# First stage of a two-block transformer kernel: 1024-column pieces of the modulation weights, sums of squares on TensorE

## The reference

```python
mod = jax.nn.silu(c) @ ada_w + ada_b                  # c: (1, 1024), ada_w: (1024, 6144)
sh_m, sc_m, g_m, sh_f, sc_f, g_f = jnp.split(mod, 6, axis=-1)
h = rms_norm(x, mix_pre_norm) * (1 + sc_m) + sh_m     # mean of x*x over the 1024 columns
proj = h @ w_in
```

## Time and profile before

| | us |
|---|---|
| median of 3 runs (lowest, highest) | 2764.87 (2758.59, 2766.57) |
| profiled execution, its own time | 2762.08 |
| span of that execution in the trace | 2759.1 |
| PE busy | 2668.9 (97%) |
| start of the stage after the first | 41.5 |

### The profile page before, as it was taken

One profiled execution on the slowest core, in us unless ns is written; L12 is line 12 of the kernel. 1 busy time (PEld: TensorE's weight loads), 2 busy tenths in 40 slices (PEclk: granted clock), 3 DMA queues, 4 the chain that ended last, 5 costly groups with the idle time before them and its releaser, 6 DMA issues. The chain is left out here.

```text
span 2759.1 us, 48978 instructions
## 1 busy us (share of the span) xinstructions
PE 2668.9 (97%) x19134; PEld 2281.0 (83%) x19134; DVE 1884.4 (68%) x3427; ACT 1205.4 (44%) x2294; POOL 285.1 (10%) x217
## 2 busy tenths in 40 slices
PE   7988899999999999999999999999999999999998
PEld 5868766778888789998878999989999857899997
DVE  3454668552332588887457888888888767788885
ACT  3232235531212454445256544465444438654444
POOL 2000114422111300001401000010000100100000
PEclk9999889999999999999999999999999999999999
DMA  8250310123232223334303333332333331323331
GB/s 279 63 169 16 111 38 5 62 77 107 92 95 88 77 77 97 110 92 124 92 17 92 89 104 96 104 107 86 109 99 101 83 86 26 92 79 113 92 108 54
DMA packets 369540, 248.89 MB, mean 90 GB/s; under 512 B 28692, under 2 KB 364376, under 8 KB 369312
## 3 DMA queue, kind: packets, MB, share of 16 engines
q1 hardware_dynamic: 368818, 245.18, 30.2%
q10 hardware_dynamic: 494, 0.59, 0.1%
HBM read 241.52 MB, written 2.12 MB: 88 GB/s over the span
## 5 line engine op out<-in xcount | busy, mean ns | idle before, releaser
L3018 ACT CAST dense_wt_hi<-ring 128x512 fp32r<-128x512 f32 x719 | 444.4, 621 | 462.5 <-PE bank L3068 220.5
L3023 DVE TENSOR_TENSOR dense_wt_lo<-ring,dense_wt_hi 128x512 fp32r<-128x512 f32 x719 | 493.6, 689 | 105.8 <-ACT dense_wt_hi L3018 104.4
L3055 PE MATMUL bank<-dense_operand_hi,dense_wt_hi 128*128 128x256 f32 x1248 | 353.7, 283 | 4.2 <-DVE h L3672 4.2
L3057 PE MATMUL bank<-dense_operand_hi,dense_wt_lo 128*128 128x256 f32 x1248 | 353.1, 283 | 0.0
L3056 PE MATMUL bank<-dense_operand_lo,dense_wt_hi 128*128 128x256 f32 x1248 | 353.1, 283 | 0.0
L3068 PE MATMUL bank<-dense_act_hi,dense_wt_hi 128*128 128x512 f32 x832 | 258.4, 392 | 0.8 <-DVE dense_act_lo L3336 0.8
L3068 PE MATMUL bank<-dense_act_lo,dense_wt_hi 128*128 128x512 f32 x832 | 257.1, 390 | 0.0
L3068 PE MATMUL bank<-dense_act_hi,dense_wt_lo 128*128 128x512 f32 x832 | 256.7, 390 | 0.0
L3055 PE MATMUL bank<-feat_hi,dense_wt_hi 128*128 128x256 f32 (+1 forms) x820 | 246.8, 301 | 7.5 <-DVE h L3707 3.2
L3055 PEld LDWEIGHTS bank<-dense_operand_hi,dense_wt_hi 128*128 128x128 f32 x1248 | 238.8, 191 | 12.2 <-issue 5.0
L3057 PE MATMUL bank<-feat_hi,dense_wt_lo 128*128 128x256 f32 (+1 forms) x820 | 245.8, 300 | 0.0
(11 more groups left out here) (726 smaller groups left out, 5429.3 us busy)
## 6 DMA issues: line engine op xcount, KB each, us to landing
ring<-in_ffn_w_up SPq DMA_DIRECT2D x88, 512.0 KB, 3.9
ring<-in_ffn_w_gate SPq DMA_DIRECT2D x88, 512.0 KB, 5.2
ring<-in_ffn_w_down SPq DMA_DIRECT2D x60, 512.0 KB, 4.8
ring<-in_ada_w SPq DMA_DIRECT2D x24, 1024.0 KB, 8.0
ring<-in_ffn_w_down SPq DMA_DIRECT2D x52, 256.0 KB, 3.9
ring<-in_w_ffn_gate SPq DMA_DIRECT2D x11, 1024.0 KB, 5.3
ring<-in_w_ffn_up SPq DMA_DIRECT2D x11, 1024.0 KB, 5.4
ring<-in_w_in SPq DMA_DIRECT2D x8, 1024.0 KB, 6.5
```

Source lines behind the costliest of these rows:

```text
L3018: self.nc.scalar.copy(self.hi(i), src).then_inc(self.s_high, 1)
L3023: self.nc.vector.tensor_tensor(self.lo(i), self.items[i][1], self.hi(i).bitcast(F32), ALU.subtract).then_inc(self.s_low, 1)
L3055: pe.matmul(out, h[:, w], xh, start=start and k == 0, stop=False, skip_group_check=shared)
L3057: last = pe.matmul(out, l[:, w], xh, start=False, stop=stop and k == 3, skip_group_check=shared)
```

## The change

`FirstModulation` takes the place of `Modulation` in the first stage (the later use of `Modulation` stays). A chunk is now 256 rows by 1024 columns, contiguous pieces of 4 KB; four chunks in a row add up to 1024 of the sums, in one PSUM bank, and a chunk is four products over 512 columns. Two turns of four products each, with two moving columns that pick the rows below and above partition 64, take the place of eight turns of two. DVE clears the two banks in place of the products with zeros. DVE copies all eight tiles of `x`. GpSimd has nothing to do in the stage; PE sums all eight tiles of squares, 32 products. The table of the root is loaded by ACT ahead of its first copy, and the fillers are in other places.

```diff
--- before.py
+++ after.py
@@ -1005,6 +1005,55 @@
             v.tensor_tensor(coef[:, 32:40], mod[:, 40:48], par("ffn_post_norm"), ALU.mult)
 
 
+class FirstModulation:
+
+    def __init__(self, K, st, name, banks, turned):
+        self.K, self.nc, self.banks, self.turned = K, K.nc, banks, turned
+        self.seg = K.plan.segments[name]
+        self.row = st.sb("row", [P, 2, T])
+        self.s_silu, self.s_row, self.s_turned, self.s_clear = st.sems("silu_c", "row_out", "row_turned", "mod_cleared")
+
+    def chunk(self, pe, r):
+        K = self.K
+        K.wait_loaded(pe, self.seg["n0"] + r)
+        w = K.raw(self.seg["n0"] + r).rearrange("p (k n) -> p k n", n=D)
+        for g in range(4):
+            k, half = g % 2, g // 2
+            last = pe.matmul(K.bank[self.banks[r // 4]][32 * g:32 * g + 1, :], K.coef[:, 2 * (r % 4) + k:2 * (r % 4) + k + 1],
+                             w[:, k, half * T:(half + 1) * T], start=r % 4 == 0, stop=r % 4 == 3)
+        last.then_inc(K.tiles_done, 1)
+
+    def turn(self, pe, b):
+        K = self.K
+        pick = K.k("heads").rearrange("p (h d) -> p h d", d=HD)[:, :, 0]
+        pe.wait_ge(self.s_row, b + 1)
+        for j in range(4):
+            last = pe.matmul(K.bank[self.turned][:, 8 * b + j:8 * b + j + 5:4], self.row[:, b, j * P:(j + 1) * P], pick, start=True, stop=True)
+        last.then_inc(self.s_turned, 1)
+
+    def silu(self):
+        K = self.K
+        self.nc.scalar.activation(K.coef[:, 0:8], K.par[:, COL["c"]:COL["c"] + 8], ACT.Silu).then_inc(self.s_silu, 1)
+
+    def clear(self):
+        for b in self.banks:
+            self.nc.vector.memset(self.K.bank[b][:, :], 0.0).then_inc(self.s_clear, 1)
+
+    def row_out(self, act, b):
+        K = self.K
+        act.wait_ge(K.tiles_done, self.seg["mark0"] + 4 * b + 4)
+        self.nc.scalar.copy(self.row[:, b, :], K.bank[self.banks[b]][:, :]).then_inc(self.s_row, 1)
+
+    def vector(self, dve):
+        K, v, mod, coef = self.K, self.nc.vector, self.K.mod, self.K.coef
+        dve.wait_ge(self.s_turned, 2)
+        v.tensor_tensor(mod[:, 0:16], K.bank[self.turned][:, 0:16], K.par[:, 0:16], ALU.add)
+        dve.drain()
+        v.scalar_tensor_tensor(coef[:, 8:16], mod[:, 8:16], 1.0, K.par[:, COL["mix_pre_norm"]:COL["mix_pre_norm"] + KD], ALU.add, ALU.mult)
+
 def start_stage(K):
 
 
@@ -1012,12 +1061,11 @@
     with stage(K, "start") as st:
         rows = st.sb("rows", [P, 2, P])
         xin = st.sb("xin", [P, TB, D])
-        s_ident, s_x, s_zero, s_a, s_b, s_par, s_xt, s_xv, s_xa = st.sems(
-            "ident", "x_in", "zero", "rows_a_turned", "rows_b_turned", "par", "x_turned", "x_vector", "x_scalar")
+        s_ident, s_x, s_zero, s_a, s_b, s_par, s_xt, s_xv, s_sq, s_sum = st.sems(
+            "ident", "x_in", "zero", "rows_a_turned", "rows_b_turned", "par", "x_turned", "x_vector", "x_squared", "x_summed")
         s_rows, n_rows = st.sems("rows_a", "rows_b"), [0, 0]
-        M = Modulation(K, st, "mod1", 0)
-        nxt = SumOfSquares(K, st, "next", tiles_of(K.x), tiles_of(K.h), 4)
-        R = Rstd(K, st, "norm", 4, 6, D, nxt)
+        M = FirstModulation(K, st, "mod1", (6, 7), 5)
+        R = Rstd(K, st, "norm", 4, 6, D)
         early = CONST["freq"][1]
 
         def rows_in(e, which, group):
@@ -1046,28 +1094,14 @@
                 rows_in(act, 0, ROWS_A)
                 act.wait_ge(s_par, 1)
                 M.silu()
-                def copies(ks):
-                    for k in ks:
-                        act.wait_ge(s_xt, k + 1)
-                        nc.scalar.copy(K.x[:, k, :], K.bank[k % 4][:, :]).then_inc(s_xa, 1)
-
-                def squares(ks):
-                    for k in ks:
-                        act.wait_ge(s_xa if k % 2 else s_xv, k // 2 + 1)
-                        nxt.square(k)
-
-                for r in range(4):
-                    M.row_out(act, r)
-                copies((1, 3))
-                squares(range(4))
-                M.row_out(act, 4)
-                copies((5, 7))
-                squares((4, 5))
-                M.row_out(act, 5)
-                squares((6, 7))
-                M.row_out(act, 6)
+                nc.scalar.activation(K.warm[:, :], K.k("eps")[:, 0:1], ACT.Sqrt)
+                M.row_out(act, 0)
+                for k in range(KD):
+                    act.wait_ge(s_xv, k + 1)
+                    nc.scalar.activation(K.h[:, k, :], K.x[:, k, :], ACT.Square).then_inc(s_sq, 1)
+                act.wait_ge(s_sum, 1)
                 R.root(act)
-                M.row_out(act, 7)
+                M.row_out(act, 1)
 
             @block.vector
             def _(dve):
@@ -1075,7 +1109,7 @@
                 M.clear()
                 dve.wait_ge(s_a, 1)
                 nc.vector.tensor_copy(K.par[:, 0:N_A], K.bank[0][:, 0:N_A]).then_inc(s_par, 1)
-                for k in range(0, KD, 2):
+                for k in range(KD):
                     dve.wait_ge(s_xt, k + 1)
                     nc.vector.tensor_copy(K.x[:, k, :], K.bank[k % 4][:, :]).then_inc(s_xv, 1)
                 dve.wait_ge(s_b, 1)
@@ -1084,37 +1118,55 @@
                 nc.vector.tensor_copy(K.x_squares, K.bank[4][:, 0:TB])
                 M.vector(dve)
 
-            @block.gpsimd
-            def _(pool):
-                nxt.add(pool, nc.gpsimd)
-
             @block.tensor
             def _(pe):
                 def turn_x(ks):
                     pe.wait_ge(s_x, 16 * TB)
                     for k in ks:
                         if k >= 4:
-                            pe.wait_ge(s_xa if k % 2 else s_xv, k // 2 - 1)
+                            pe.wait_ge(s_xv, k - 3)
                         for t in range(TB):
                             last = pe.transpose(K.bank[k % 4][:, t * P:(t + 1) * P], xin[:, t, k * P:(k + 1) * P], K.k("ident"))
                         last.then_inc(s_xt, 1)
 
                 def turn_b():
                     pe.wait_ge(s_rows[1], 16 * n_rows[1])
-                    pe.wait_ge(s_xv, 4)
+                    pe.wait_ge(s_xv, 5)
                     pe.transpose(K.bank[0][:, 0:N_B], rows[0:N_B, 1, :], K.k("ident")[0:N_B, 0:N_B]).then_inc(s_b, 1)
 
-                def columns():
-                    K.keep_clock(pe, K.bank[2], 4)
-                    nxt.columns(pe)
-                    K.keep_clock(pe, K.bank[2], 2)
+                def columns(ks):
+                    for k in ks:
+                        pe.wait_ge(s_sq, k + 1)
+                        for b in range(TB):
+                            last = pe.matmul(K.bank[4][:, b:b + 1], K.h[:, k, b * P:(b + 1) * P], K.k("ones")[:, 0:1],
+                                             start=k == b == 0, stop=k == KD - 1 and b == TB - 1)
+                    if k == KD - 1:
+                        last.then_inc(s_sum, 1)
 
                 pe.wait_ge(s_ident, 16)
                 pe.wait_ge(s_rows[0], 16 * n_rows[0])
                 pe.transpose(K.bank[0][:, 0:N_A], rows[0:N_A, 0, :], K.k("ident")[0:N_A, 0:N_A]).then_inc(s_a, 1)
                 pe.wait_ge(s_par, 1)
-                M.tensor(pe, {3: lambda: turn_x(range(4)), 4: lambda: turn_x(range(4, 8)), 5: turn_b, 6: columns, 7: lambda: R.spread(pe)})
-                K.keep_clock(pe, K.bank[2], 2)
+                pe.wait_ge(M.s_clear, 2)
+                pe.wait_ge(M.s_silu, 1)
+                for r in range(4):
+                    M.chunk(pe, r)
+                K.keep_clock(pe, K.bank[2], 8)
+                turn_x(range(4))
+                M.turn(pe, 0)
+                M.chunk(pe, 4)
+                turn_x(range(4, 8))
+                M.chunk(pe, 5)
+                columns(range(4))
+                M.chunk(pe, 6)
+                turn_b()
+                columns(range(4, 8))
+                K.keep_clock(pe, K.bank[2], 4)
+                R.spread(pe)
+                M.chunk(pe, 7)
+                K.keep_clock(pe, K.bank[2], 4)
+                M.turn(pe, 1)
+                K.keep_clock(pe, K.bank[2], 4)
         K.norm_value = R.value
 
 
@@ -4025,7 +4077,8 @@
         plan.add(name, 34, lambda c: ffn_chunk(*parts, c))
 
     w_in = io["w_in"][0]
-    plan.add("mod1", 8, cols(io["ada_w"][0], 0, WC), marks=1, split=False)
+    ada_w = io["ada_w"][0].rearrange("(k p) n -> p k n", p=P)
+    plan.add("mod1", 8, lambda c: ada_w[:, 2 * (c % 4):2 * (c % 4) + 2, D * (c // 4):D * (c // 4 + 1)], marks=1, split=False)
     plan.add("in_q", 1, cols(w_in, 0, WC))
     plan.add("in_kv", 1, cols(w_in, O_KV, P), marks=1)
     plan.add("in_rkv", 6, cols(w_in, O_R, WC))

```

## The result

| | before | changed |
|---|---|---|
| median of 14 runs each, us | 2762.16 | 2769.68 |
| lowest run | 2755.16 | 2765.42 |
| profiled execution, own time (span) | 2762.08 (2759.1) | 2772.76 (2770.9) |
| first instruction of the stage after the first | 41.5 | 50.3 |

The ratio is 1.0027, 95% interval [1.0018, 1.0036]: the changed kernel is about 7.5 us slower. (One run of before took 3770 us and is left out of the ratio.) The forecast was +0.5, which it counted among the differences that cannot be told from none. The time lies in the range, at 0.27%, but the interval excludes a change of nothing, and the mechanism in the trace is one that the prediction did not have. By the prediction's own sign, a stage's end moved by more than 8 us (it moved by 8.8), it was wrong as a whole; that the number lies in the range is luck.

What follows compares the result with a forecast made beforehand. Transfers bound the first stage up to chunk 6, then GpSimd, then PE's own list. Chunk 4 at 23.54 plus 18.25 gives 41.79 against 41.25: net +0.5 us, median 2765.4, range 2757 to 2773.

Steps and rivals of the forecast that it cites:

- the prediction's own sign: Prediction wrong as a whole if the first stage's end moves over 8 us or a later stage changes length.
- Transfers: First-stage loads: 4 KB pieces at 409 GB/s, a chunk 2.56 us for 3.03, chunk 4 landing 2.33 us earlier.
- the unchanged rate: Rival: early loads stay near 346 GB/s despite longer pieces; +3.1 us, total 2768.0; chance 0.25.
- A chunk: Four PE products over 512 columns replace eight over 256 and still take 0.97 us; bounds 0.49 and 3.23.
- the serial products: Rival: a chunk's four wide products run one after the other, 3.23 us a chunk; +16 us, total 2781; chance 0.04.
- Turns: Each new turn on PE has 8 records in place of 4 and takes 0.94 us, for 0.47.
- copies and squares: DVE's eight copies (0.69 each) and ACT's eight squares (0.55 each) stay hidden, by 3.5 us.
- PE before `x`: Zero products go; chunk 0 about 1.9 us, chunks 1 to 3 about 1.0 each, fillers to 19.2, `x` at 19.7.
- The sum from chunk 4: PE's work from chunk 4 to the stage's end: 18.25 us with no late transfers, from 23.54 to 41.79.
- The columns: PE's 32 column products replace GpSimd's additions: 64 records at 0.113, 7.24 us against 1.81.
- SyncE's last transfers: Chunk 7's slot comes free at about 38.5, so the last `w_in` load and remaining constants do not move.
- Outside the stage: Case: a difference from something outside the first stage, of either sign; chance 0.07.

Runs made afterwards that it cites:

- wide columns: The changed kernel with its 32 column products given 128 moving columns of ones in place of one; median 2763.13 us, ratio 1.0002 to the kernel before.
- again: The changed kernel run once more, unaltered, for a second trace; median 2770.15 us, ratio 1.0024 to the kernel before.
- columns alone: The kernel before with GpSimd's additions replaced by 32 one-column products on PE, pieces still 1 KB; median 2774.65 us, ratio 1.0049, four runs.

## Why the prediction was right and wrong

- *Transfers: right.* Forecast 409 GB/s, measured 409; the unchanged rate (25 in 100) is out. Chunk 4 was forecast to start at 23.54 and did at 24.07 (23.68 to 24.14 in the others with 4 KB pieces), for 25.87 before. The Trainium skill's figures in "DMA: Bandwidth & Descriptors", Specifications, read as in the prediction (line rate from 512 B on, about 358 GB/s from HBM), do not hold here: 346, 385 and 409 for 1, 2 and 4 KB.
- *A chunk: right*, 0.97; the serial products are out. *Turns* 0.8 to 0.9 (forecast 0.94), *copies and squares* hidden, as forecast.
- *PE before `x`*: 5.25 for four chunks (forecast 4.9; up to 6.4 in the other traces), filler to 20.21; PE, not `x`, was late by about half a microsecond, hidden behind chunk 4.
- *The sum from chunk 4: right at clock 1.00*, 18.25 forecast to the end of the last filler, 18.11 in "wide columns" (23.87 to 41.98), which as a whole came out at 1.0002.
- *The columns: wrong.* The failed step is "In their place come 32 column products, 64 records at 0.113 (16 from 35.35 to 37.16): 7.24, against 1.81." It takes the distance of 16 records that ran for 1.8 us between fillers and multiplies it by four, at an assumed clock of 1.00. Measured: 11.7 (4.93 + 6.77); chunk 6 between the two halves, and filler, spread and chunk 7 behind them, ran at half pace too. In all 7.9 us were lost from chunk 4 to the next stage. With 128 columns, where the clock held, the 64 records took 7.4 (3.77 + 3.61), so the price of a record was right and the clock was not. I had read the fall of the clock after 1.63 us without work as a matter of idle time only, and with PE's list free of gaps saw no danger. None of the rivals had this loss either; the range covers it because it was widened for other reasons.
- *SyncE's last transfers*, forecast not to move (about 38.5), did: the rest of the constants was issued at 47.64, for 39.30 before, behind the end of chunk 7 (47.10).
- *Outside the stage* nothing systematic is seen; behind the stage the profiled executions differ from the one of before by -3.0 to +4.1 us, with falls of the clock after 165 us that differ from execution to execution.

## What to carry to other kernels

A TensorE that the profile shows as busy without a gap can still lose its clock: here a long row of products with one moving column fell to 1.2 GHz in all three traces that had one, and long rows with 128 columns kept 2.4 GHz in all three. Where a product costs nearly the same with one moving column as with 128, as here (3.67 and 3.77 us for 32 records), give a long row of them 128; for 16 records the gain is not shown. And where a term of a sum is a row multiplied up, ask whether the longer run keeps the state in which the row was taken.

## What the runs showed of the hardware

- The granted clock went from 1.00 to 0.50 some 2.2 us (30.1, changed kernel), 4.6 us (32.3, again) and 3.8 us (39.8, "columns alone") after the first of a row of one-column products (64 records, in two of the traces with a chunk in their middle) without idle time, and came back 5.6, 3.2 and 10.9 us after the row's end, when fillers, spread and in two of the traces a chunk had run. The Trainium skill, "TensorE: Matmul & The Clock Gate", section What's actually happening, says that activity releases the throttle and that the monitor looks at how busy PE is; the traces agree only if "busy" there is not the profile's: in the profile PE is 100% busy over these rows.
- Rates of a single core's loads from 6 to 10 us, by contiguous piece: 346 GB/s (1 KB), 385 (2 KB), 403 to 410 (4 KB). From 346 and 409 follows, as an estimate, a fixed 9.7 ns for each piece on one of 16 engines beside 435 GB/s for its bytes, and the middle rate came out as worked out from these. That a piece has a fixed cost is a form that fits three rates, not a shown cause.
- Larger pieces also free SyncE: issuing the first four chunks took 2.10 us in place of 6.23 (2.31 with pieces of 2 KB).
